# 32 KB rows for the expert weights, and a last pair whose down product ends on 1 MB: a four-layer decoder with two mixtures of experts

## What is computed

```python
g_logits = (hf @ w_group + b_group).astype(jnp.float32)
g_top = jnp.argmax(g_logits, axis=-1)            # one of 4 groups
e_prob = jax.nn.softmax(e_logits, axis=-1)       # 8 experts of that group
top_p, top_j = lax.top_k(e_prob, MOE_TOP_K)      # 2 experts for each token
...
xb = h_pad[tok]
hidden = jax.nn.silu(xb @ w_gate[e]) * (xb @ w_up[e])
return (hidden @ w_down[e]) * gt[:, None]
```

## Time and profile before

| | us |
|---|---|
| median of 3 runs (1543.56 to 1544.81) | 1543.92 |
| span of the profiled execution, first to last instruction | 1546.3 |
| TensorE busy | 1310.8 (85%) |
| VectorE busy | 463.5 (30%) |
| ScalarE busy | 278.2 (18%) |
| GpSimd busy | 266.4 (17%) |
| HBM read | 495.11 MB, 322 GB/s over the span |
| share of the chain that ended last: TensorE, DMA, SP's queue | 27%, 27%, 17% |

### The profile page before, as it was taken

One profiled execution on the slowest core, in us unless ns is written; L12 is line 12 of the kernel. 1 busy time (PEld: TensorE's weight loads), 2 busy tenths in 40 slices (PEclk: granted clock), 3 DMA queues, 4 the chain that ended last, 5 costly groups with the idle time before them and its releaser, 6 DMA issues.

```text
span 1546.3 us, 22323 instructions
## 1 busy us (share of the span) xinstructions
PE 1310.8 (85%) x9344; PEld 705.8 (46%) x9344; DVE 463.5 (30%) x904; ACT 278.2 (18%) x545; POOL 266.4 (17%) x158
## 2 busy tenths in 40 slices
PE   9999999999999998667667767999999676666676
PEld 5754466547878654223223224755644232232232
DVE  2554663654845521111001001286311010010011
ACT  2142410433321210300000000215211110111010
POOL 0675236640000008780000000000000000000000
PEclk9999999999999999987988999999899989899889
DMA  9922452336431799999999999945699999999997
GB/s 372 365 114 82 192 227 76 153 138 273 165 130 37 278 405 403 427 428 429 429 428 427 428 429 428 375 164 237 263 420 426 426 429 427 427 428 426 428 427 318
DMA packets 45444, 498.20 MB, mean 322 GB/s; under 512 B 6720, under 2 KB 9536, under 8 KB 13120
## 3 DMA queue, kind: packets, MB, share of 16 engines
q1 hardware_dynamic: 45376, 497.22, 78.1%
HBM read 495.11 MB, written 2.10 MB: 322 GB/s over the span
## 4 chain that ended last, share of the span: by engine, by line
PE 27%; DMA 27%; SPq 17%; DVE 2%; issue 1%; ACT 1%; DVEq 0%; ACTq 0%
DMA weight_ring<-in_moe_weights 24%; SPq L2918 17%; PE banks L3132 6%; PE banks L331 3%; DMA x_normed<-in_moe_weights 3%; PE banks L1768 2%; PE banks L1961 2%; PE banks L3143 2%; PE banks L2564 2%; PE banks L3107 1%; PE banks L2473 1%; PE banks L1310 1%; PE banks L3118 1%; PE banks L1893 1%; PE banks L3177 1%
## 5 line engine op out<-in xcount | busy, mean ns | idle before, releaser
L3132 PE MATMUL banks<-weight_ring,arena 128*32 128x512 f32 x1472 | 220.2, 731 | 123.8 <-DMA weight_ring<-in_moe_weights 123.7
L3050 DVE TENSOR_TENSOR arena<-arena,banks 64x512 f32<-64x512 f32 x32 | 22.1, 690 | 657.9 <-ACT arena L2973 657.9
L3132 PEld LDWEIGHTS banks<-weight_ring,arena 128*32 128x32 f32 x1472 | 45.9, 122 | 280.4 <-issue 140.3
L3107 PE MATMUL banks<-arena,x 128*128 128x64 f32 x960 | 112.3, 276 | 0.0
L3107 PEld LDWEIGHTS banks<-arena,x 128*128 128x128 f32 x960 | 112.0, 195 | 0.0
L2973 ACT ACTIVATE arena<-banks 64x512 f32<-64x512 f32 x32 | 18.9, 590 | 500.8 <-PE banks L3132 500.8
L3143 PE MATMUL banks<-weight_ring,arena 128*32 128x512 f32 x728 | 86.5, 600 | 19.7 <-issue 8.1
L978 POOL TENSOR_TENSOR weight_ring<-spare_weights,weight_ring 128x2048 f32<-128x2048 f32 x16 | 74.0, 4637 | 71.0 <-DVE arena L822 38.5
L3177 PE MATMUL banks<-arena 64*128 64x512 f32 x240 | 59.6, 615 | 21.0 <-ACT arena L2979 21.0
L3132 PE MATMUL banks<-arena 128*32 128x512 f32 x352 | 58.5, 684 | 16.3 <-DMA arena<-in_moe_weights 16.1
L331 PE MATMUL banks<-weight_ring,hT 128*128 128x512 f32 x128 | 56.3, 595 | 0.0
(11 more groups left out here) (561 smaller groups left out, 1955.8 us busy)
## 6 DMA issues: line engine op xcount, KB each, us to landing
weight_ring<-in_moe_weights SPq DMA_DIRECT2D x137, 2048.0 KB, 26.8
weight_ring<-in_ring_weights SPq DMA_DIRECT2D x35, 2048.0 KB, 12.7
arena<-in_moe_weights SPq DMA_DIRECT2D x18, 2048.0 KB, 43.9
spare_weights<-in_moe_weights SPq DMA_DIRECT2D x10, 2048.0 KB, 44.5
mix<-in_moe_weights SPq DMA_DIRECT2D x9, 2048.0 KB, 47.5
arena<-in_moe_weights SPq DMA_DIRECT2D x17, 1024.0 KB, 43.4
x_normed<-in_moe_weights SPq DMA_DIRECT2D x9, 1024.0 KB, 40.4
hT<-in_moe_weights SPq DMA_DIRECT2D x9, 1024.0 KB, 46.3
```

What stands on the lines that cost most here:

```text
L3107: ins = pe.matmul((b_x, b_dn)[k // 4][:, k % 4 * 2 * CAP:(k % 4 + 1) * 2 * CAP], g.x[:, tt, k * P:(k + 1) * P], Pr[:, tt, :], start=(tt == ...
L3132: ins = pe.matmul(b_gu[q:q + CAP, :], xg[:, 2 * quarter + k, e * CAP:(e + 1) * CAP], up_w(where, quarter, e)[:, which, k, :], start=(quart ...
```

## The change

The weights of an expert pair now lie in DRAM as three tiles of 4 MB (two slots side by side, rows of 32 KB). Where both slots of a tile go to neighbouring buffers, one load fetches both. So that they are neighbours, x_normed, hT and mix become one buffer (`wide`), the spare slot and the arena another, the arena's parts change places, and ring slots are counted one further on from chunk `N_LOW`. The wide loads begin with pair 3 of each layer. `load_later` waits until both slots of a tile have been used. For odd pairs (`alone`) slot 4 stays a load of 2 MB and slot 5 becomes two loads of 1 MB.

The down weights are split by output columns: slot 4 holds columns 0 to 511, slot 5 the others, in two halves by hidden rows. `down_half` leaves the products of the two 128-row parts of a half in different partitions of a PSUM bank, and the adding product sums over all 128 partitions. ScalarE copies each column half on its own. In the last pair the first column half is multiplied, copied and added before TensorE waits for the last 1 MB. VectorE adds the banks in the order 0, 2, 1, 3, and in layer 0 ScalarE squares the first two before it copies the second column half.

```diff
+N_LOW = DEPTH * (KT + 5) + 7
+MOE_SLOTS = (4, 5, 0, 1, 2, 3)
...
-        return i % SLOTS
+        return (i if i < N_LOW else i + 1) % SLOTS
...
+        later_wide = [moe_ring_wide(g, c0), moe_ring_wide(g, c0)]
         lag = 1
     else:
-        second = extra + [[g.spare], [router.xT_flat, g.xs_flat]]
+        wide = [g.arena[:, EXTRA_AT:EXTRA_AT + 2 * SW], g.wide[:, :], g.spare_wide]
+        second = [[wide[j // 2][:, (j % 2) * SW:(j % 2 + 1) * SW]] for j in range(SLOTS)]
         third = first
         later = [first, second]
+        later_wide = [moe_ring_wide(g, c0), wide]
         lag = 2
+    early = [[2] * SLOTS, [1, 1, 1, 1, 2, 1] if ly == 0 else [1, 1, 2, 1, 1, 1]]
+    alone = ((), (4, 5))
...
-    def down_w(where, j, e):
+    def down_w(where, j, half):
 
         parts = where[j]
-        w = parts[e] if len(parts) == 2 else parts[0][:, e * 2048:(e + 1) * 2048]
-        return w.rearrange("p (f n) -> p f n", f=2)
+        w = parts[half] if len(parts) == 2 else parts[0][:, half * 2048:(half + 1) * 2048]
+        return w.rearrange("p (e f n) -> p e f n", e=2, f=2)
...
+        def load_alone(pair, j):
+
+            if j == 4:
+                load(later[1], 1, pair, j)
+            else:
+                for half, sem in enumerate((landed[1][j], half_landed)):
+                    at = slice(half * 2048, (half + 1) * 2048)
+                    sp.dma_start(later[1][j][0][:, at], moe_piece(A, ly, pair, j)[:, at]).then_inc(sem, 16)
+
+        def load_later(bank, pair, n, more):
+
+            for d in range(SLOTS // 2):
+                if 2 * d in alone[bank]:
+                    for j in (2 * d, 2 * d + 1):
+                        released(j, n, more)
+                        load_alone(pair, j)
+                else:
+                    released(2 * d + 1, n, more)
+                    sp.dma_start(later_wide[bank][d], A["moe_weights"][ly, pair, d]).then_inc(landed[bank][2 * d], 16)
 
         if ly == 0:
             released(0, 0, 1)
@@ -2926,34 +2962,29 @@
                 else:
                     released(0, 0, 2)
                 load(third, 0, 2, j)
-            for j in range(SLOTS):
-                if j == 0:
-                    released(5, 0, 2)
-                else:
-                    released(j - 1, 0, 3)
-                load(later[1], 1, 3, j)
-                if j == 0:
+            released(5, 0, 2)
+            for d in range(2):
+                released(2 * d, 0, 3)
+                sp.dma_start(later_wide[1][d], A["moe_weights"][ly, 3, d]).then_inc(landed[1][2 * d], 16)
+                if d == 0:
                     for dst, name in ((g.s5.B[:, 0], "s5_b"), (g.s5.C[0], "s5_c"), (g.s5.bT, "s5_bT")):
                         sp.dma_start(dst, A[name]).then_inc(g.s5_bc_landed, 16)
+            for j in alone[1]:
+                released(j - 1, 0, 3)
+                load_alone(3, j)
         else:
             for j in range(SLOTS):
                 released(j, 0, 1)
                 load(third, 0, 2, j)
-            for j in range(SLOTS):
-                released(j, 0, 2)
-                load(later[1], 1, 3, j)
+            load_later(1, 3, 0, 2)
         T = turns(sp)
         with sp.Fori(0, T) as t:
             with sp.Fori(0, NP // 2 - 2) as i:
                 for bank in range(2):
-                    for j in range(SLOTS):
-                        released(j, t * NP + i * 2, 5 + bank - lag)
-                        load(later[bank], bank, i * 2 + (4 + bank), j)
+                    load_later(bank, i * 2 + (4 + bank), t * NP + i * 2, 5 + bank - lag)
...
-        def of_pair(n):
-            act.wait_ge(s_gu, n * 4 + 4)
+        def of_pair(done, last=False):
+            act.wait_ge(s_gu, done * 4)
             act.activation(sil[0:2 * CAP, :], b_gu[0:2 * CAP, :], ACT.Silu).then_inc(s_sl, 1)
-            act.wait_ge(s_Pt, n + 1)
+            act.wait_ge(s_Pt, done)
             act.copy(PT, b_t[:, S:2 * S]).then_inc(s_PTc, 1)
-            act.wait_ge(s_ht, n + 1)
+            act.wait_ge(s_ht, done)
             act.copy(hidT, b_t[:, 0:8 * CAP].rearrange("p (f j) -> p f j", f=4)).then_inc(s_hc, 1)
-            act.wait_ge(s_dn, n + 1)
-            act.copy(y, b_dn[:, :]).then_inc(s_yc, 1)
+            act.wait_ge(s_da, done)
+            act.copy(ys[0], b_down[0]).then_inc(s_yc[0], 1)
+            if last and ly == 0:
+                act.activation(g.small[:, 410:412], router.rstd, ACT.Sqrt)
+                squares(0)
+                squares(1)
+            act.wait_ge(s_dn, done)
+            act.copy(ys[1], b_down[1]).then_inc(s_yc[1], 1)
+
+        def squares(i):
+            act.wait_ge(s_add, i + 1)
+            g.n_odd.squares(act, ADD_ORDER[i] // 2, ADD_ORDER[i] % 2)
...
-            act.activation(g.small[:, 410:412], router.rstd, ACT.Sqrt)
-            for tt in range(TT):
-                for ch in range(2):
-                    act.wait_ge(s_add, 2 * tt + ch + 1)
-                    g.n_odd.squares(act, tt, ch)
-                g.n_odd.root(act, tt)
+            for i in (2, 3):
+                squares(i)
+                g.n_odd.root(act, ADD_ORDER[i] // 2, squared=i + 1)
...
-        added(0)
-        added(1)
-        if ly == 0:
-            g.n_odd.eps(dve, 0)
-        added(2)
-        if ly == 0:
-            dve.wait_ge(s_add, 2)
-            g.n_odd.scale(dve, 0)
-        added(3)
+        for i, j in enumerate(ADD_ORDER):
+            added(j)
+            if ly == 0 and i == 1:
+                g.n_odd.eps(dve, 0, squared=1)
+                g.n_odd.eps(dve, 1, squared=2)
         dve.wait_ge(s_add, 4)
         if ly == 0:
-            g.n_odd.eps(dve, 1)
-            g.n_odd.evacuate(dve, 0)
-            g.n_odd.scale(dve, 1)
-            g.n_odd.evacuate(dve, 1)
+            for tt in range(TT):
+                g.n_odd.scale(dve, tt)
+                g.n_odd.evacuate(dve, tt)
...
-        def down(half, where, bank, rounds):
-            arrived(where, bank, 4 + half, rounds)
+        def down_half(nh, half, where):
+            w = down_w(where, 4 + nh, half)
             for f in range(2):
-                for nh in range(2):
-                    for e in range(2):
-                        q = (2 * nh + e) * CAP
-                        ins = pe.matmul(b_dn[q:q + CAP, :], hidT[:, 2 * half + f, e * CAP:(e + 1) * CAP],
-                                        down_w(where, 4 + half, e)[:, f, nh * 512:(nh + 1) * 512],
-                                        start=(half == 0 and f == 0), stop=(half == 1 and f == 1), tile_position=(0, q))
+                for e in range(2):
+                    q = (2 * f + e) * CAP
+                    ins = pe.matmul(b_down[nh][q:q + CAP, :], hidT[:, 2 * half + f, e * CAP:(e + 1) * CAP], w[:, e, f, :],
+                                    start=(half == 0), stop=(half == 1), tile_position=(0, q))
             return ins
+
+        def last_half_arrived(rounds):
+            pe.wait_ge(half_landed, rounds * 16 + 16)
+
+        def down(nh, where, bank, rounds):
+            if rounds is None:
+                arrived_early(bank, 4 + nh)
+                if nh and bank == 1:
+                    pe.wait_ge(half_landed, 16)
+            else:
+                arrived(bank, 4 + nh, rounds)
+                if nh and bank == 1:
+                    last_half_arrived(rounds)
+            down_half(nh, 0, where)
+            return down_half(nh, 1, where)
+
+        def add_rows(nh, opens=False):
+            for tt in range(TT):
+                pe.matmul(ps[2 * tt + nh][:, :], PT[:, tt * P:(tt + 1) * P], ys[nh], start=opens, stop=True,
+                          skip_group_check=True).then_inc(s_sum[2 * tt + nh], 1)
...
-            down(1, later[1], 1, rounds).then_inc(s_dn, 1)
-            pe.wait_ge(s_yc, pairs)
-            for tt in range(TT):
-                for nh in range(2):
-                    r = slice(nh * 2 * CAP, (nh + 1) * 2 * CAP)
-                    pe.matmul(ps[2 * tt + nh][:, :], PT[r, tt * P:(tt + 1) * P], y[r, :], start=False, stop=True,
-                              skip_group_check=True).then_inc(s_sum[2 * tt + nh], 1)
+            arrived(1, 5, rounds)
+            down_half(1, 0, later[1])
+            pe.wait_ge(s_yc[0], pairs)
+            add_rows(0)
+            last_half_arrived(rounds)
+            down_half(1, 1, later[1]).then_inc(s_dn, 1)
+            pe.wait_ge(s_yc[1], pairs)
+            add_rows(1)
 
         gather_first(0)
         gather_first(1)
-        of_pair(0, first, 0, 1, opens=True)
-        of_pair(1, second, 1, 1)
-        of_pair(2, third, 0, 2)
+        of_pair(0, first, 0, None, opens=True)
+        of_pair(1, second, 1, None)
+        of_pair(2, third, 2, None)
         T = turns(pe)
         with pe.Fori(0, T * (NP // 2) - 2) as i:
-            of_pair(i * 2 + 3, later[1], 1, i + 2)
-            of_pair(i * 2 + 4, later[0], 0, i + 3)
-        of_last(T * NP, T * (NP // 2))
+            of_pair(i * 2 + 3, later[1], 1, i + 1)
```

(38 more changed lines are left out.)

159 lines of the change are left out of this document (83 added, 76 removed).

## The result

The changed kernel takes 1552.49 us (median of 4 runs, 1551.91 to 1553.09), the kernel before 1544.37 beside it (4 runs). The ratio is 1.0043, 95% interval 1.0029 to 1.0056: slower by about 6.6 us by the ratio (8.1 by the two medians), where 1545.9 and no change was forecast. The profiled execution took 1552.13 us, for a span of 1550.0.

What follows compares the result with a forecast made beforehand. Expert-weight streaming by DMA was taken to bound the two mixtures. Rate -5.4, idle DMA +3.2, ends +1.2 and +3.0 gave +2.0 us: 1548.3 for the span, 1545.9 as timed, no change; 8-in-10 range 1540.8 to 1550.8.

Steps and rivals of the forecast that it cites:

- The rate term: Weight streams of both layers: fewer, longer rows save 10.6 ns per row on each engine, together -5.4 us.
- the first rival: Weight streams: long rows save nothing, since rows from 512 B run at line rate; +7.4 us, 1551.3, slower; 13%.
- The step on the adding products: Mixture pairs: the wider contraction lies hidden under the stream; one adding product costs 0.5 us.
- the hidden copy: Pairs 0 and 1, layer 0: copying the first column half during the second saves TensorE 0.70 us each, 1.4 together.
- The idle term: Layer 0, pair 3's first load: waiting for pair 2's first quarter leaves DMA idle 4.5 us instead of 1.3, +3.2 us.
- The end of layer 1: Behind layer 1's last landing: quarters 2 and 3 start later under one tile, last add ends at 1543.6, +1.2 us.
- the rival on the clock: Last pairs: the longer wait before quarter 2 lowers TensorE's clock, +2 to +4 us on the sum, 1548 to 1550; 13%.
- The rival that foresaw shorter ends: Behind last landings: layer 1 ends 2.1 us earlier, layer 0 1.5, if quarter 3 starts promptly; 1538.1, faster; 5%.
- The end of layer 0: Behind layer 0's last landing: first transpose moves from 977.50 to 980.5, +3.0 us.
- the hold of the second copy: Layer 0's end, ScalarE: squarings drawn forward delay the second column half's copy by 1.2 us.

Runs made afterwards that it cites:

- wide_only: Kernel before, with only wide weight rows in even pairs and odd pairs' slots 0 and 1, pair 3's first tile in two loads: 1540.89 us, ratio 0.996.
- adding_128: Kernel before, with only the adding products' contraction widened from 64 to all 128 partitions (sums not the reference's): 1548.79 us, ratio 1.0015.
- before_again: Kernel before, unchanged, run for a second profile: 1544.44 us, ratio 0.999.
- pair3_split: Changed kernel, with pair 3's first tile in layer 0 in two loads, the first waiting for pair 1 alone: 1549.93 us, ratio 1.0021.
- three_undone: Changed kernel, with pair 3's first tile in two loads, odd pairs' slots 2 and 3 loaded singly, and squares behind the second copy: 1542.36 us, ratio 0.9977.
- odd_slots: Changed kernel, with slots 2 and 3 of odd pairs each in their own load: 1546.92 us, ratio 1.0006.

## Why the prediction was wrong

*The rate term held.* Forecast -5.4 us. A round of layer 0 fell from 58.74 to 58.46, one of layer 1 from 58.91 to 58.45; over six and a half rounds each that is -1.8 and -3.0, together -4.8. In the DMA's records one row of 32 KB takes 1,217 ns on its engine and one of 16 KB 615, so 13 ns are saved for two rows made one; the 10.6 ns taken from the two layers' difference had the size. (435 is 1.5% above 428.4 and not 1.6%; nothing rests on it.) By the rule taken from the Trainium skill ("DMA: Bandwidth & Descriptors", Specifications), where rows over 512 B all run at line rate (the first rival), nothing would be saved; the trace does not agree, by 13 ns for two rows. wide_only shows the gain in the time.

*The step on the adding products failed.* The prediction said that "the wider contraction of the adding product lie[s] under the stream", took 0.5 us for one adding product, 1.0 for the two of a column half, and let TensorE gain 0.70 us per pair from the hidden copy. The 59.6 us for 120 products was read as the price of products in turn; it was that of two at a time, on different halves of the partitions. On 128 partitions a record is as long as before (606 ns for 615) but has no partner, so the four products of a pair, eight records, take 3.70 us (adding_128), and the two of a column half 1.98. The copy is hidden as forecast (the idle time before these products falls from 21.0 us to 1.7), and yet a pair of TensorE's own pace became 0.95 us longer instead of 0.70 shorter: from the first quarter of pair 0 to that of pair 2 it takes 40.79 us after and 38.89 in before_again. The Trainium skill states the mechanism ("TensorE: Matmul & The Clock Gate", the section on why this matters for your kernels): products over fewer than 128 rows, sliced so that they lie in different row groups, run concurrently. The trace agrees, with 59.6 us for 111.0.

*The idle term was too small by half.* Forecast +3.2; the traces have +5.1 against the first profile and +6.1 against the second. The time of issue was right within 0.4 us by two errors against each other: the profile of before began the mixture some 3 us late, by 10.2 us at the lower clock that no later profile has there (pair3_split and three_undone have 3.4 us), and TensorE was taken as 3.3 us too quick over two pairs. (A span lies some 2.1 us below the time of its execution, 1540.7 for 1542.87 and 1550.0 for 1552.13, so that first execution took about 1548.4 us, an estimate, and was not 2.4 but some 4 us slower than the median.) The wait itself was read rightly: pair3_split took it away and got 3.4 us back.

*The end of layer 1 was too small.* Forecast +1.2, measured +4.0. The chain's form was right: quarter 2 at 1526.28 (1526.3 forecast), but quarter 3 at 1531.30 for 1529.8, by 1.65 us of the lower clock, so the rival on the clock was right at this place. The two adding products of the first column half took 1.98 us for 1.0, and the last two 1.98 again, before VectorE's last add. odd_slots shows that the tile of slots 2 and 3 is the cause: with it undone the end is 0.6 us shorter than before instead of 4.0 longer. The rival that foresaw shorter ends named quarter 3 as what decides, and three_undone bears it out in kind but not in size: 0.6 us shorter in layer 1, where it had set 2.1, and 0.1 in layer 0, where it had set 1.5.

*The end of layer 0* was forecast at +3.0 and came at +3.3 (10.7 for 7.4), near it, but not as it was worked out. Inside it the hold of the second copy was 0.4 us and not 1.2, because the block that it waits for came 1 us later, behind longer products.

Summed by its own terms the forecast would have been -4.8, +5.1 to +6.1, +4.0 and +3.3, between +7.6 and +8.6 us, where the medians show +8.1. Part of that is luck: layer 1 won 1.9 us up to its last landing, not 3.0. Its rate term is there in full, since from the landing of pair 5 to that of pair 14 after takes 262.9 us and before_again 265.0, 0.23 less a pair. But in after the last pair lands 30.1 us behind its predecessor, where before_again has 29.4 and the other kernels with wide rows 29.3. In those the start differs instead: pair 4 has landed 232.0 to 233.9 us behind layer 0's transpose in the six kernels with wide rows, after 232.2 in before_again. Why, no run separates.

## What to carry to other kernels

A weight stream at the DMA's full rate still gains from longer rows, some 13 ns for every two rows made one, but a longer tile lands whole: keep it away from the first load after a queue has run low and from the tiles of the last pair, where something behind a landing waits for each part. Before a product's contraction is widened, see in the timeline how long the group of products takes and not one of them: products of equal length may have run beside each other. And profile the kernel before twice: what one execution does at a clock stretch can move a start by 3 us and leave idle time in the kernel before, against which the change's own looks small.

## What was not expected of the hardware

Two products over 64 partitions each, on different halves, cost about as much together as one over 128: 8 records in 1.99 us against 8 in 3.70, with the single one at 615 and 606 ns. And of two profiles of the unchanged kernel one has TensorE for 10.2 us at the lower clock at each router and the other has not, with spans of 1546.3 and 1540.7 us.
